# High and low value parts side by side in one attention matmul, added by VectorE

## The chip, the cores and the metric

The kernel runs on one core of a Trainium2 chip. The metric is device time of one launch in microseconds (us). TensorE (PE in the profile), VectorE (DVE), ScalarE (ACT), GpSimd (POOL) and SyncE (SP, here only a queue of transfers) each run their own instruction list and meet at semaphores.

## The reference

One decoder layer over 1024 rows of width 1024, in float32: attention, then an MLP, then a gated embedding. Only the attention is touched:

```python
q, k, v = split(rmsnorm(x, g) @ wqkv)          # 16 query heads, 4 key/value heads, head width 64
q, k = rmsnorm(q, gq), rmsnorm(k, gk)
# blocks of 128 rows; block n sees the keys of blocks n-1 and n, window 128
probs = exp(scores - m) / (sum + exp(sink - m))
o = einsum('bnkgqs,bnskd->bnqkgd', probs, vb)  # the step that the change rewrites
mix = o.reshape(b, s, H * HD) @ wo
```

The output has to agree with a float32 computation, so every operand of a matmul is split into a high part (rounded to the engine's fp32r type) and a low part (the rest), and a product is three matmuls: high x high, high x low, low x high.

## The kernel before

The attention is worked off in 8 blocks n of 128 rows. Each has four steps j, one for each key/value head with its four query heads; (n, j) is one step. The whole program is written by hand: each engine has its own list, a semaphore stands between any two that hand something on, and blocks 1 to 5 are a loop in every list. Blocks 0, 6 and 7 are written out.

What TensorE does in step j of block n: `scores` of (n, j); a piece of the projections of block n+1 (`project`, L1919: "q0" and "q8" are the two halves of the queries, "k" is keys and values); `weigh_values` (L1990, the product of probabilities and values) two steps behind, so of (n, j-2); and `turn_probs` (L1969, transposes) of (n, j-1). In step 3 it starts `project("q8")` of the next block, which waits until VectorE has scaled the keys (L1326), since "k" and "q8" share a PSUM bank. That start is called the **gate** below, since it comes once in a block.

VectorE in a step: `add_bias` (L1374, L1387, L1392: masks and biases the scores and takes their maximum), the step's share of the norms (L1308 sums of squares, L1321 and L1326 scaling) and of the low parts (L1301, L1344, L1335), `scale_probs` (L1404), and then `pT_lo_part` (L1410, low part of the turned probabilities of the step before). In step 0 `v_diff` (L1354) follows, in step 1 `v_lo_part` (L1360 and L1363, the low parts of the block's values and of their difference to the block before).

ScalarE: `exps` (L938, waits for the maxima), squares (L891), high parts (L928 queries, L920 keys, L947 probabilities), and `attention_out` (L955), which copies the finished 128x256 product of (n, j-2) out of its PSUM bank just ahead of `pT_hi_part` (L947).

GpSimd: the inverse square roots (L691, L693), the mask on the turned probabilities (`mask_probs`, L760 for the high part, L763 for the low), and `dv_hi_part` (L737), the high part of the difference of values. In its list `dv_hi_part` stands behind `head_norm("q0")` of the next block. VectorE's L1363 waits for it.

The values lie in `vz` as [slot, part, head, 64] with zeros between the heads, so that 128 columns from it hold one head's 64 values and 64 zeros, on either side. Twelve matmuls of 256 columns make one product: two slots (this block's values and the difference), three passes, and two placements. The upper 64 partitions of the bank take two of the four query heads and the lower 64 the other two. The bank `pv_bank` is used by all steps in turn, so the product of the next step waits for `attended`, which the copy signals.

Of the kernel before, what the change touches and what calls it, by code (L numbers as in the profile page):

```python
# [30 lines left out]
P = 128  # L31
# [30 lines left out]
def trunk_layer(nc, x, p, mix_g, mlp_g, ple_g, wqkv, gq, gk, sinks, wo, w1, w2, w_proj, w_gate, out):  # L62
# [31 lines left out]
    with ExitStack() as ctx:  # L94
# [55 lines left out]
        vz = sb("vz", [P, 2, 2, (2 * KV + 1) * HD], F32R, in_a)  # L150
# [168 lines left out]
        half_ready = sem("half_ready")  # L319
# [14 lines left out]
        gain_zero = sem("gain_zero")  # L334
# [33 lines left out]
        pv_done = sem("pv_done")  # L368
        attended = sem("attended")
# [293 lines left out]
        def _(pool):  # L663
            pool.memset(gain[:, 0:2 * P], 0.0).then_inc(gain_zero, 1)
            pool.memset(half[:], -0.5).then_inc(half_ready, 1)
# [4 lines left out]
            pool.wait_ge(half_ready, 1)  # L670
# [24 lines left out]
            pool.memset(vz[:].bitcast(F32), 0.0).then_inc(zeros_ready, 1)  # L695
# [49 lines left out]
            def dv_hi_part(b):  # L745
# [4 lines left out]
                copy(vz[:, 0, HI, HD:(2 * KV + 1) * HD].rearrange("p (v a d) -> p v a d", v=KV, a=2)[:, :, 0, :],  # L750
# [23 lines left out]
            def body(n, last=False):  # L774
# [61 lines left out]
        def _(act):  # L836
# [65 lines left out]
            def values(slot, s):  # L902
                return vz[:, slot, s, HD:(2 * KV + 1) * HD].rearrange("p (v a d) -> p v a d", v=KV, a=2)[:, :, 0, :]

            def v_hi_part(b):
                act.wait_ge(v_staged, b + 1)
                if isinstance(b, int) and b == 0:
                    act.wait_ge(zeros_ready, 2)

                wait(act, pv_done, 4 * b)  # L910
                nc.scalar.activation(values(1, HI), vnext[:].rearrange("p (v d) -> p v d", v=KV),
                                     ACT.Copy).then_inc(v_hi, 1)
# [36 lines left out]
            def attention_out(n, j):  # L949
# [91 lines left out]
            act.wait_ge(gain_zero, 1)  # L1041
# [5 lines left out]
            act.wait_ge(half_ready, 1)  # L1047
# [236 lines left out]
        def _(dve):  # L1284
# [63 lines left out]

            def v_diff(b):
                dve.wait_ge(v_staged, b + 1)  # L1350
                if isinstance(b, int) and b == 0:
                    dve.wait_ge(zeros_ready, 3)
# [3 lines left out]
            def v_lo_part(b):  # L1356
                def values(slot, s):
                    return vz[:, slot, s, HD:(2 * KV + 1) * HD].rearrange("p (v a d) -> p v a d", v=KV, a=2)[:, :, 0, :]
# [949 lines left out]
```

## Time and profile before

| | us |
|---|---|
| median of three runs | 1116.42 |
| lowest and highest | 1115.62, 1116.71 |
| the profiled execution | 1118.16 |
| its span in the trace | 1116.4 |
| attention, start to the gate of block 7 | 246.3 |
| one block of the loop, gate to gate | 31.4 |

The profiled execution took 1.8 us more than its span, and 1.7 us more than the median. A difference worked out in the trace is taken over to the median as it is. Times below are us from the start of the span. A row of a timeline or of the chain is: start, length, engine, line, operation, output<-input and shape, how many; in brackets how long the engine stood idle before and who ended that.

### The profile page before, as it was taken

The numbers are of one execution on the slowest core, as the hardware profiler recorded it, in microseconds if no ns is written. First come the engines' busy times: TensorE is split into PE (matmuls) and PEld (weight loads), VectorE is DVE, ScalarE is ACT, GpSimd is POOL, SyncE is SP. The second block draws the span as 40 slices with busy tenths as digits, with TensorE's granted clock in tenths as the row PEclk, the third lists the DMA queues.
The fourth block names the chain that finished last, engine by engine and source line by source line (L and its number), as shares of the span: only waits on it lengthen the run. The fifth ranks groups of instructions, "written<-read, shape, count | busy, mean of one in ns | idle before, by whom it ended". The sixth has DMA issues, their size and how long they took to land.

```text
span 1116.4 us, 14894 instructions
## 1 busy us (share of the span) xinstructions
PE 1089.0 (98%) x5272; PEld 913.1 (82%) x5272; DVE 735.2 (66%) x1130; ACT 428.2 (38%) x776; POOL 148.9 (13%) x272
## 2 busy tenths in 40 slices
PE   7899999998999999999999999999999999999998
PEld 5788888887888888888888888888888888888886
DVE  6677776777544499876677667498777863664311
ACT  7456555565423233313322343453333331243100
POOL 6543444443100000000000000000000000010000
PEclk9999999998999999999999999999999999999999
DMA  7000000121152407343353244998888872111210
GB/s 264 20 20 19 19 1 19 38 111 79 38 170 80 147 1 256 139 171 132 119 201 139 88 188 164 396 411 297 293 287 294 282 250 76 38 38 57 88 45 38
DMA packets 61361, 153.88 MB, mean 138 GB/s; under 512 B 4720, under 2 KB 5752, under 8 KB 61304
## 3 DMA queue, kind: packets, MB, share of 16 engines
q1 hardware_dynamic: 61280, 153.12, 38.4%
q8 instruction: 35, 0.57, 0.2%
q14 instruction: 22, 0.18, 0.1%
q10 hardware_dynamic: 24, 0.01, 0.0%
HBM read 119.03 MB, written 34.08 MB: 137 GB/s over the span
## 4 chain that ended last, share of the span: by engine, by line
PE 81%; DVE 8%; issue 4%; ACT 3%; POOL 2%; ACTq 0%; DVEq 0%; POOLq 0%
PE pair L2204 24%; PE pair L2184 21%; PE pair L2056 8%; PE pair L2247 8%; PE pair L1919 6%; PE pair L2224 4%; PE pair L2142 3%; PE pair L1990 2%; PE pair L2260 2%; ACT probs L938 2%; PE pair L2112 1%; PE pair L1958 1%; DVE probs L1387 1%; ACT kn L891 1%; POOL k_rstd L693 1%
## 5 line engine op out<-in xcount | busy, mean ns | idle before, releaser
L2204 PE MATMUL pair<-uT 128*128 128x512 f32 x1176 | 266.7, 389 | 0.0
L2204 PEld LDWEIGHTS pair<-uT 128*128 128x128 f32 x1176 | 220.7, 188 | 45.8
L1919 PE MATMUL pair<-WA,xT 128*128 128x512 f32 x384 | 97.4, 403 | 11.8 <-DVE kn L1326 7.8
L1193 ACT ACTIVATE uT<-wo_raw 128x1024 fp32r<-128x1024 f32 x63 | 64.3, 1055 | 105.7 <-PE pair L2204 92.7
L1735 DVE TENSOR_TENSOR uT<-wo_raw,uT 128x1024 fp32r<-128x1024 f32 x63 | 75.0, 1222 | 39.3 <-ACT uT L1193 39.2
L675 POOL TENSOR_SCALAR row_var<-row_ssq 128x1 f32<-128x1 f32 x16 | 3.1, 193 | 700.3 <-ACT hn L1092 700.3
L1919 PEld LDWEIGHTS pair<-WA,xT 128*128 128x128 f32 x384 | 70.7, 191 | 29.3 <-issue 13.2
L2056 PE MATMUL pair<-WA,oT 128*128 128x512 f32 x384 | 91.8, 397 | 2.6 <-DVE WA L1491 2.1
L2056 PEld LDWEIGHTS pair<-WA,oT 128*128 128x128 f32 x384 | 72.2, 191 | 17.8 <-issue 3.1
L2184 PE MATMUL pair<-WA,WB 128*128 128x512 f32 x336 | 78.2, 389 | 0.4 <-ACT xr L1168 0.4
L2184 PEld LDWEIGHTS pair<-WA,WB 128*128 128x128 f32 x336 | 63.0, 188 | 13.8 <-DVE WB L1669 0.8
L938 ACT ACTIVATE probs<-probs,nmax 128x129 f32<-128x129 f32 x128 | 50.0, 393 | 59.8 <-DVE nmax L1392 59.6
L2184 PE MATMUL pair<-uT,WB 128*128 128x512 f32 x240 | 56.1, 389 | 0.0
L1990 PE MATMUL pair<-pT,vz 128*128 128x256 f32 x384 | 53.3, 289 | 0.5 <-DVE pT L1410 0.5
L2184 PEld LDWEIGHTS pair<-uT,WB 128*128 128x128 f32 x240 | 45.0, 188 | 9.6 <-issue 0.2
L1990 PEld LDWEIGHTS pair<-pT,vz 128*128 128x128 f32 x384 | 50.4, 194 | 2.2 <-DVE pT L1410 0.7
L1867 DVE TENSOR_TENSOR act_buf<-pair,act_buf 128x512 f32<-128x512 f32 x16 | 11.0, 690 | 55.3 <-PE pair L2260 55.3
L1919 PE MATMUL pair<-WB,xT 128*128 128x512 f32 x192 | 45.3, 391 | 2.1 <-DVE WB L1292 2.1
L1826 DVE TENSOR_TENSOR RES<-RES,pair 128x512 f32<-128x512 f32 x48 | 30.8, 682 | 22.2 <-PE pair L2204 22.2
L2224 PE MATMUL pair<-WA 128*128 128x512 f32 x192 | 45.4, 393 | 0.0
L2247 PE MATMUL pair<-WB,uT 128*128 128x512 f32 x192 | 45.2, 391 | 0.0
L2247 PE MATMUL pair<-WA,uT 128*128 128x512 f32 x192 | 44.8, 389 | 0.0
(203 smaller groups left out, 1877.9 us busy)
## 6 DMA issues: line engine op xcount, KB each, us to landing
wo_raw<-in_m_w SPq DMA_DIRECT2D x53, 512.0 KB, 6.5
wo_raw<-hid_kept SPq DMA_DIRECT2D x36, 512.0 KB, 4.7
hid_kept<-RES SPq DMA_DIRECT2D x28, 512.0 KB, 2.6
emb<-in_m_w SPq DMA_DIRECT2D x20, 512.0 KB, 6.2
RES<-in_m_w SPq DMA_DIRECT2D x8, 1024.0 KB, 6.8
uT_f<-in_m_w SPq DMA_DIRECT2D x6, 1024.0 KB, 6.7
act_buf<-hid_kept SPq DMA_DIRECT2D x11, 512.0 KB, 4.9
hn<-in_m_w SPq DMA_DIRECT2D x11, 512.0 KB, 5.9
```

The costliest lines, as they stand in the source:

```text
L938: ex = nc.scalar.activation(row, row, ACT.Exp, bias=nmax[:, i, r:r + 1], accum_out=denom[:, i, r:r + 1])
L1193: nc.scalar.activation(operand(t, which, HI), unit(t, which), ACT.Copy).then_inc(op_hi, 1)
L1735: nc.vector.tensor_tensor(operand(t, which, LO), unit(t, which), operand(t, which, HI).bitcast(F32), ALU.subtract).then_inc(op_ready, 1)
L1826: nc.vector.tensor_tensor(RES[:, b, cols], RES[:, b, cols], bank[:], op).then_inc(posted, 1)
L1919: mm = nc.tensor.matmul(proj_bank[X][:], xT[:, s, kt, :], w[:, m, kt, at:at + BANK], start=(kt == 0 and i == 0), stop=(kt == KT - 1 and i ...
L1990: mm = nc.tensor.matmul(pv_bank[:, 0:2 * P], vz[:, kt, s, at:at + 2 * HD], pT[:, m, kt, odd * 2 * P:(odd + 1) * 2 * P], start=(done == 0), ...
L2056: mm = nc.tensor.matmul(out_bank(b, odd, c)[:], oT[:, hf, s, k % 4 * P:(k % 4 + 1) * P], wo_s[:, m, k, c * BANK:(c + 1) * BANK], start=(k ...
L2142: mm = nc.tensor.matmul(ps[i % 4][:], w1_s[:, s, kt, m * P:(m + 1) * P], uT[:, r, kt, th * BANK:(th + 1) * BANK], start=(kt == 0 and q == ...
L2184: mm = nc.tensor.matmul(chain[:, m, :], a_slot[q % 4][:, s, k, m * P:(m + 1) * P], right(i)(r)[:, k, :], start=(opens and k == 0 and n == ...
L2204: mm = nc.tensor.matmul(ps[4 * (j % 2) + m][:], operand(t, 0, s)[:, k, m * P:(m + 1) * P], operand(t, 1, r)[:, k, :], start=(g == 0 and k ...
L2224: mm = nc.tensor.matmul(ps[4 + a % 4][:], hid[:, s, k, b * P:(b + 1) * P], w2_s[:, r, k, c * BANK:(c + 1) * BANK], start=(k == 0 and q == ...
L2247: mm = nc.tensor.matmul(ps[4 + s % 2][:], uT[:, u, kt, b * P:(b + 1) * P], w[:, m, kt, :], start=(kt == 0 and q == 0), stop=(kt == KT - 1 ...
```

## The change

- `vz` becomes [slot, head, part, 64]: a head's high and low values stand side by side, and the zeros are gone (with GpSimd's clearing of `vz`). Filler keeps the other tiles where they were.
- `weigh_values` issues four matmuls of 512 columns: slot x {high, low part of the probabilities}. The upper 64 partitions of the bank then hold the product with the high values, the lower 64 that with the low values, for all four query heads. The product low x low, which was left out, is in it.
- ScalarE copies the upper half out in two instructions of 64x256: the second writes to the lower 64 partitions of RES. VectorE's new `add_lows` adds the lower half of the bank to it, also in two instructions of 64x256. It stands behind `pT_lo_part` in each step, and signals `attended`.
- In GpSimd's `body`, `dv_hi_part` moves ahead of `head_norm("q0")`. Block 0 keeps its order.
- Two semaphores of the start become one.

```diff
-                copy(vz[:, 0, HI, HD:(2 * KV + 1) * HD].rearrange(...)[:, :, 0, :],
+                copy(vz[:, 0, :, HI, :],
                      vprev[:].rearrange("p (v d) -> p v d", v=KV)).then_inc(dv_moved, 1)
...
                 place_sinks(n, 2)
+                dv_hi_part(n)
                 if not last:
                     head_norm("q0", n + 1)
-                dv_hi_part(n)
...
-                nc.scalar.activation(dst, pv_bank[:, 0:2 * P], ACT.Copy).then_inc(attended, 1)
+                nc.scalar.activation(dst[0:HD, :], pv_bank[0:HD, 0:2 * P], ACT.Copy)
+                nc.scalar.activation(dst[HD:P, :], pv_bank[0:HD, 2 * P:4 * P], ACT.Copy).then_inc(pv_copied, 1)
...
+            def add_lows(n, j):
+                dve.wait_ge(pv_copied, 4 * n + (j + 1))
+                dst = RES[:].rearrange("p b n -> p (b n)")[:, bass.ds(n * D + j * 2 * P, 2 * P)]
+                nc.vector.tensor_tensor(dst[0:HD, :], pv_bank[HD:P, 0:2 * P], dst[0:HD, :], ALU.add)
+                nc.vector.tensor_tensor(dst[HD:P, :], pv_bank[HD:P, 2 * P:4 * P], dst[HD:P, :],
+                                        ALU.add).then_inc(attended, 1)
...
                     if not (first and j < 1):
                         pT_lo_part(t - 1, (j - 1) % 2)
+                    if not (first and j < 2):
+                        add_lows(*before(n, j, 2))
...
-                    for s, m in PASSES:
-                        for odd in range(2):
-                            at = 2 * HD * j + (0 if odd else HD)
-                            mm = nc.tensor.matmul(pv_bank[:, 0:2 * P], vz[:, kt, s, at:at + 2 * HD],
-                                                  pT[:, m, kt, odd * 2 * P:(odd + 1) * 2 * P],
-                                                  start=(done == 0), stop=(done == 11))
-                            done += 1
+                    for m in (HI, LO):
+                        mm = nc.tensor.matmul(pv_bank[:], vz[:, kt, j, :, :].rearrange("p s d -> p (s d)"),
+                                              pT[:, m, kt, :], start=(done == 0), stop=(done == 3))
+                        done += 1
```

On VectorE, step 1 of the loop, before: the scaled probabilities, the low part of the turned ones, and the two low parts of the values.

```order
L1404 TENSOR_TENSOR probs<-probs,rden 128x4x128
L1410 TENSOR_TENSOR pT<-pair,pT 128x512
L1360 TENSOR_TENSOR vz<-vnext,vz 128x4x64
L1363 TENSOR_TENSOR vz<-vprev,vz 128x4x64
L431 ISA
L1374 COPY_PREDICATED pair<-current,pair 128x2x128
```

The same place after the change:

```order
L1410 TENSOR_TENSOR probs<-probs,rden 128x4x128
L1416 TENSOR_TENSOR pT<-pair,pT 128x512
L1348 REGISTER_ALU
L1350 ISA
L1350 TENSOR_TENSOR RES<-pair,RES 64x256
L1351 ISA
L1351 TENSOR_TENSOR RES<-pair,RES 64x256
L1366 TENSOR_TENSOR vz<-vnext,vz 128x4x64
L1369 TENSOR_TENSOR vz<-vprev,vz 128x4x64
L432 ISA
L1380 COPY_PREDICATED pair<-current,pair 128x2x128
```

Two additions stand between the low part of the probabilities and what followed it; steps 0, 2 and 3 have them at the same place.

On GpSimd, in the middle of the loop, before (vz<-vprev is `dv_hi_part`):

```order
L771 TENSOR_SCALAR probs<-sink 128x4
L691 TENSOR_SCALAR q_var<-q_ssq,row_eps 128x8
L693 TENSOR_TENSOR q_rstd<-q_var,half 128x8
L737 TENSOR_SCALAR vz<-vprev 128x4x64
L760 AFFINE_SELECT pT<-pT 128x512
```

And after:

```order
L771 TENSOR_SCALAR probs<-sink 128x4
L737 TENSOR_SCALAR vz<-vprev 128x4x64
L692 TENSOR_SCALAR q_var<-q_ssq,row_eps 128x8
L694 TENSOR_TENSOR q_rstd<-q_var,half 128x8
L760 AFFINE_SELECT pT<-pT 128x512
```

The copy now comes ahead of the norm of the queries instead of behind it.

## Rows read from the trace of the kernel before

**Rows 1.** The page, part 1: busy time of TensorE over the span.
```profile
PE 1089.0 (98%) x5272; PEld 913.1 (82%) x5272; DVE 735.2 (66%) x1130; ACT 428.2 (38%) x776; POOL 148.9 (13%) x272
```

**Rows 2.** Busy time, blocks 1 and 3, gate to gate: stretch, length, engines' busy, PEclk, DMA.
```profile
56.28:89.36 33.08, 31.93 (x189) 28.08 (x189) 22.77 (x73) 17.56 (x55) 15.15 (x28) 0.95 0.05 17
120.80:152.25 31.45, 30.30 (x188) 26.94 (x189) 22.87 (x73) 17.46 (x55) 14.04 (x24) 1.00 0.05 17
```

**Rows 3.** The chain, gate of block 3 to the next: start, length, what.
```profile
130.66 1.44 PE pair L1990 x12
...
133.48 3.43 PE pair L1919 x15
...
142.52 0.70 DVE pT L1410
...
145.54 0.48 DVE pair L1374 x2
```

**Rows 4.** Timeline around the values' low parts and xT, block 3.
```profile
131.84 1.29 DVE L1301 TENSOR_TENSOR xT<-pair,xT 128x512 fp32r<-128x512 f32 x2
...
133.32 3.59 PE L1919 MATMUL pair<-WA,xT 128*128 128x512 f32 x15
...
143.13 0.41 DVE L1360 TENSOR_TENSOR vz<-vnext,vz 128x256 fp32r<-128x256 f32 x1
...
144.78 0.83 DVE L1363 TENSOR_TENSOR vz<-vprev,vz 128x256 fp32r<-128x256 f32 x1 [1.24 <-POOL vz L737]
```

**Rows 5.** Timeline of VectorE and ScalarE after the gate at 152.25.
```profile
152.83 0.68 DVE L1410 TENSOR_TENSOR pT<-pair,pT 128x512 fp32r<-128x512 f32 x1
153.44 0.75 DVE L1374 COPY_PREDICATED pair<-current,pair 128x256 f32<-128x256 uint32 x2
...
157.07 0.69 ACT L920 ACTIVATE kT<-pair,columns 128x512 fp32r<-128x512 f32 x1
...
158.62 0.39 ACT L955 ACTIVATE RES<-pair 128x256 f32 x1 [0.87 <-PE pair L1990]
...
158.92 0.60 ACT L947 ACTIVATE pT<-pair 128x512 fp32r<-128x512 f32 x1
159.55 0.69 DVE L1410 TENSOR_TENSOR pT<-pair,pT 128x512 fp32r<-128x512 f32 x1 [0.78 <-ACT pT L947]
...
160.94 0.69 DVE L1308 TENSOR_REDUCE q_ssq<-kn 128x8 f32<-128x512 f32 x1 [0.70 <-ACT kn L891]
```

**Rows 6.** Timelines: runs on the same partitions, runs that change them; maxima of step 1.
```profile
13.85 2.81 DVE L1292 SCALAR_TENSOR_TENSOR WA<-RES,columns,WA 128x512 fp32r<-128x512 f32 x4 [0.26 <-ACT WA L846]
...
16.11 2.55 ACT L846 ACTIVATE WA<-RES,columns 128x512 fp32r<-128x512 f32 x4
...
137.07 0.16 DVE L1392 SCALAR_TENSOR_TENSOR nmax<-rmax,nsink 128x4 f32<-128x4 f32 x1
...
137.47 1.39 ACT L928 ACTIVATE qT<-pair,gq_s 64x512 fp32r<-64x512 f32 x2 [2.10 <-PE pair L1943]
...
155.39 1.53 DVE L1344 SCALAR_TENSOR_TENSOR qT<-pair,gq_s,qT 64x512 fp32r<-64x512 f32 x2
```

**Rows 7.** Timeline of TensorE in block 7: a wait, and what follows.
```profile
269.42 2.90 PE L2056 MATMUL pair<-WA,oT 128*128 128x512 f32 x6 [2.06 <-DVE WA L1491]
...
272.12 2.76 PE L1990 MATMUL pair<-pT,vz 128*128 128x256 f32 x12
...
274.68 1.74 PE L2056 MATMUL pair<-WA,oT 128*128 128x512 f32 x6
```

**Rows 8.** Busy time in stretches ahead of a gate: PE busy second, PEclk third from the end.
```profile
53.20:56.28 3.08, 0.72 (x5) 0.45 (x5) 1.82 (x5) 2.37 (x7) 1.90 (x3) 1.00 0.00 0
...
150.40:152.25 1.85, 0.70 (x6) 0.45 (x5) 0.80 (x3) 1.05 (x3) 1.59 (x2) 1.00 0.00 0
```

**Rows 9.** Timeline of GpSimd at the start.
```profile
1.77 2.02 POOL L695 MEMSET vz<- 128x2304 f32 x1
...
12.77 0.21 POOL L682 TENSOR_SCALAR row_var<-row_ssq 128x1 f32<-128x1 f32 x1 [3.95 <-ACT xn L867]
```

More of the change, by code:

```diff
@@ L149, in trunk_layer @@
         vnext = sb("vnext", [P, KV * HD], F32, in_a)
-        vz = sb("vz", [P, 2, 2, (2 * KV + 1) * HD], F32R, in_a)
+        vz = sb("vz", [P, 2, KV, 2, HD], F32R, in_a)
+        sb("after_vz", [P, 1280], F32, in_a)
         pT = sb("pT", [P, 2, 2, BANK], F32R, in_a)
@@ L318, in trunk_layer @@
         ident_ready = sem("ident_ready")
-        half_ready = sem("half_ready")
         zeros_ready = sem("zeros_ready")
@@ L333, in trunk_layer @@
         x_eps = sem("x_eps")
-        gain_zero = sem("gain_zero")
+        small_filled = sem("small_filled")
         heads_in = sem("heads_in")
@@ L368, in trunk_layer @@
         pv_done = sem("pv_done")
+        pv_copied = sem("pv_copied")
         attended = sem("attended")
@@ L663, in _ @@
         def _(pool):
-            pool.memset(gain[:, 0:2 * P], 0.0).then_inc(gain_zero, 1)
-            pool.memset(half[:], -0.5).then_inc(half_ready, 1)
+            pool.memset(gain[:, 0:2 * P], 0.0).then_inc(small_filled, 1)
+            pool.memset(half[:], -0.5).then_inc(small_filled, 1)
             pool.memset(ident[:], 0.0).then_inc(ident_ready, 1)
@@ L669, in _ @@
                                base=0, pattern=[[-1, P]], channel_multiplier=1).then_inc(ident_ready, 1)
-            pool.wait_ge(half_ready, 1)
+            pool.wait_ge(small_filled, 2)
             def row_norm(squares, var_sem, rstd_sem, b):
@@ L749, in dv_hi_part @@
                     stand(pool, pv_done, 4 * b)
-                copy(vz[:, 0, HI, HD:(2 * KV + 1) * HD].rearrange("p (v a d) -> p v a d", v=KV, a=2)[:, :, 0, :],
+                copy(vz[:, 0, :, HI, :],
                      vprev[:].rearrange("p (v d) -> p v d", v=KV)).then_inc(dv_moved, 1)
@@ L900, in stage_v @@
                                      scale=row_rstd[:]).then_inc(v_staged, 1)
-            def values(slot, s):
-                return vz[:, slot, s, HD:(2 * KV + 1) * HD].rearrange("p (v a d) -> p v a d", v=KV, a=2)[:, :, 0, :]
             def v_hi_part(b):
                 act.wait_ge(v_staged, b + 1)
-                if isinstance(b, int) and b == 0:
-                    act.wait_ge(zeros_ready, 2)
                 wait(act, pv_done, 4 * b)
-                nc.scalar.activation(values(1, HI), vnext[:].rearrange("p (v d) -> p v d", v=KV),
+                nc.scalar.activation(vz[:, 1, :, HI, :], vnext[:].rearrange("p (v d) -> p v d", v=KV),
                                      ACT.Copy).then_inc(v_hi, 1)
@@ L1039, in oT_hi_half @@
                 nc.scalar.activation(oT[:, hf, HI, :], src, ACT.Copy).then_inc(oT_hi, 1)
-            act.wait_ge(gain_zero, 1)
+            act.wait_ge(small_filled, 1)
             act.dma_start(gain[0:KT, 0:P], mix_g.rearrange("(k p) -> k p", p=P)).then_inc(gain_in, 16)
@@ L1045, in _ @@
                               g.partition_broadcast(2).unsqueeze(0)).then_inc(heads_in, 16)
-            act.wait_ge(half_ready, 1)
+            act.wait_ge(small_filled, 2)
             nc.scalar.activation(warm[:], half[:, 0:1], ACT.Exp)
@@ L1347, in q_lo_part, with before @@
                     op1=ALU.subtract).then_inc(T_ready[X], 1)
+            def add_lows(n, j):
[4 more added lines that the diff above has]
+                                        ALU.add).then_inc(attended, 1)
+            def before(n, j, lag):
+                return (n, j - lag) if j >= lag else (n - 1, j - lag + GROUPS)
             def v_diff(b):
@@ L1351, in v_diff @@
                 if isinstance(b, int) and b == 0:
-                    dve.wait_ge(zeros_ready, 3)
+                    dve.wait_ge(zeros_ready, 2)
                 wait(dve, dv_moved, 2 * b)
@@ L1422, in last_part @@
                     v_diff(n)
+                    add_lows(n - 1, 2)
                 if j == 1:
@@ L1428, in last_part @@
                     v_lo_part(n)
+                    add_lows(n - 1, 3)
                     wo_lo_unit(2)
@@ L1434, in last_part @@
                     pT_lo_part(t - 1, (j - 1) % 2)
+                    add_lows(n, 0)
                     wo_lo_unit(4)
@@ L1438, in last_part @@
                     pT_lo_part(t - 1, (j - 1) % 2)
+                    add_lows(n, 1)
                     wo_lo_unit(5)
@@ L1533, in _ @@
             pT_lo_part(NB * GROUPS - 1, 1)
+            add_lows(NB - 1, 2)
             oT_lo_half(1, 1)
@@ L1570, in _ @@
             add_attention(0, False)
+            add_lows(NB - 1, 3)
             oT_lo_half(2, 0)
```

11 lines of the change are left out of this document (4 added, 7 removed).

## The prediction

> **What bounds the kernel now.** I read the page first. TensorE is busy 98% of the span [rows 1], so the 12 matmuls that become 4 look like a plain gain. The second view, busy time by block, says how much of that holds in the attention: a block takes 31.45 us and TensorE is busy in 30.30 of them [rows 2]. The rest is one wait at the gate. The third view, the chain of waits, says what sets the gate [rows 3]. A block has two stages. In the first, from the gate at 120.80 [rows 2] to the turn of the queries "q8", the chain lies on TensorE. In the second it leaves TensorE: ScalarE takes the turned queries, then come exponentials, squares, VectorE (L1410 at 142.52), GpSimd's copy, VectorE again (`add_bias` at 145.54) [rows 3], exponentials and key norm, up to the gate at 152.25. A matmul saved in the second stage buys nothing, while each VectorE instruction between 142.52 and 145.54 costs its full length. The reader is also to see that the first stage is TensorE's by a hair only: the low parts of xT end at 131.84 + 1.29 = 133.13, and the projection that needs them starts at 133.32 [rows 4]. So VectorE is at the edge in both stages, and it is VectorE that gets the new work.
>
> **Removed: eight of twelve matmuls.** Twelve took 1.44 us in the chain [rows 3], 0.12 each. A matmul of 512 columns took 3.43 / 15 = 0.229 [rows 3], so four take 0.92 and each product gets 0.52 shorter: 32 products, 16.6 us of TensorE's time. Two of the four in a block lie in the first stage, at most 1.04 there, and the other two lie beside the second.
>
> **Added: the pair of additions.** No row shows a 64x256 addition. Its own length is taken from L1360, 128x256, 0.41 [rows 4]; lines of this kernel take time by columns, not by partitions. What matters is how close it can follow its neighbour. From below: L1360's class starts the next one 0.34 later (my estimate, from L1410 to L1374, which start 0.61 apart at a length of 0.68 [rows 5], so 0.07 overlap), and a pair costs 0.68. From above: L1344, two instructions that swap the halves of the partitions, took 1.53 for two of 0.75 [rows 6], so the second starts 0.78 after the first and there is no overlap but a gap of 0.03; L1292 has the same operation and columns, stays on all partitions, and took 2.81 for four, 0.69 apart. `add_lows` swaps halves at each of its steps: its first reads the lower half of PSUM behind a full-height L1410, its second reads and writes the lower half of RES, and what follows is back at the top. So I take the upper value: L1410 costs 0.72 and not 0.61, each addition 0.45, together **1.01 a pair**. ScalarE shows the same: L928 with swapped halves 1.39 for two, 0.70 apart, L846 on all partitions 2.55 for four, 0.62 apart [rows 6]. So its two copies cost 0.39 each where one cost 158.92 - 158.62 = 0.30 [rows 5], 0.48 more.
>
> The Trainium skill has a rule that speaks against the change here: in "VectorE: DVE Perf Modes", section "Two Vector instructions with no wait between them", an instruction whose input or output starts in another group of 32 partitions than the one before is held until everything before it has finished. The trace agrees (0.78 against 0.69 apart). By the rule the sum is the one I make; without it, it is the first rival's.
>
> **First stage, with the additions.** From the gate at 152.25 [rows 5]: the pair of (n, 0) comes behind L1410 at 152.83, so L1374 goes from 153.44 to 154.45, and the exponentials and the keys' high part on ScalarE from 157.07 to 158.08. ScalarE is free 0.62 later, at 158.70. The product was ready 0.52 earlier, at 158.10, which is no longer what is late. Two copies, 0.78: L947 starts at 159.48, not 158.92. L1410 starts at 160.11, not 159.55, and with 0.61 + 1.01 behind it L1308 starts at 161.73, not 160.94. VectorE's idle 0.78 and 0.70 are used up and **0.79** is left over. It reaches TensorE through xT, since there was no slack (133.13 to 133.32). The third pair of the stage, in step 0, has cover: the maxima for step 1 are there at 137.07, and ScalarE is busy with the queries until 137.47 + 1.39 = 138.86 [rows 6], 1.8 later; the pair and the longer copies use 1.0 + 0.5 of it.
>
> **Second stage.** GpSimd's copy now needs only the product of (n-1, 3) and `v_diff`, both long done, so the wait of 1.24 ahead of L1363 goes [rows 4]. What is late next is VectorE itself: L1360 starts 1.01 later, at 144.14, L1363 at 144.47 and, still beside GpSimd's mask, takes 0.76 to the next: `add_bias` starts at 145.23, not 145.54, **-0.31**. ScalarE's longer copies cost nothing here: VectorE runs through from the squares' sums to L1410 at 142.52 [rows 3], and does not stand waiting for it.
>
> The length of L1363 has two bounds: 0.83 as now, or 0.41 like its twin L1360 [rows 4]. The Trainium skill, "GPSIMD Engine Reference", section "1. Specifications", says that GpSimd shares its SBUF interfaces with VectorE instructions that have two SBUF inputs, which is L1363's case; the trace agrees in that only the one of the two that starts with GpSimd's mask takes 0.83. GpSimd's mask moves to the same moment as before, so I take 0.83.
>
> **The sum.** A block: +0.79 - 0.31 = +0.48. Six periods lie between the gate at 56.28 and block 7's at 246.3. The first ran partly at half clock (33.08 us, clock 0.95 [rows 2]), TensorE is the later one in its first stage, and I take +0.1 - 0.31 = -0.2. Five others: +2.4. Block 7: three pairs, 3.0, stand on VectorE before the third low part of WO (L1491), which TensorE waits 2.06 for [rows 7]. Behind that TensorE is the bound, at half clock first: the product took 274.68 - 272.12 = 2.56, and four matmuls at the (272.12 - 269.42) / 6 = 0.45 of the six before it take 1.80 [rows 7], -0.76; two more save 0.52 each, so 3.0 - 1.8 = +1.2. The last product lies beside the turn of oT on ScalarE and VectorE, no gain; the last additions lie beside the output projection. The clearing of `vz`, 2.02, had 3.95 of idle time behind it [rows 9]: nothing. Block 0 has its first additions behind the key norm, nothing before its gate. Together -0.2 + 2.4 + 1.2 = **+3.4**. The profiled execution would be 1118.16 + 3.4 = 1121.6; the median is 1116.42 + 3.4 = **1119.8**. Nothing after the attention changes: TensorE's list is the same there.
>
> **Rivals.**
> 1. *The additions and copies overlap like full-height neighbours* (faster). A pair is 0.68, the copies 0.27 each. First stage: ScalarE is ready for L947 at 158.91, L1410 starts at 159.54 and L1308 at 160.83, -0.11. Second: -1.24 + 0.68 = -0.56. Five blocks of -0.67, block 1 -1.0 (half of TensorE's saving arrives there), block 7 3 x 0.68 - 1.8 = +0.2: -4.1, **1112.3**. For it: no row has this very form. Against it: [rows 6]. Chance 0.22.
> 2. *The copy's move also frees L1363 from the mask* (about no change). It takes 0.41: another -0.41 in six blocks, -2.5, **1117.3**. For it: GpSimd's list is shorter ahead of it. Against: the norm of the queries still ends where it did, and the mask follows at once. Chance 0.18.
> 3. *TensorE's clock falls in each block* (slower). Work pauses longer ahead of the gate. In block 0 a stretch of 3.08 us with 0.72 busy, four transposes, was followed by a fall to half clock; 1.85 us with 0.70 busy was not [rows 8]. With the products shorter that stretch becomes some 2.4 us, between the two. A fall cost 33.08 - 31.45 = 1.63 [rows 2], of which some 0.67 is covered where VectorE is late anyway: 0.96 in five blocks, +4.8, **1124.6**. It decides from the point where the pause of 2.4 counts as the 3.08 did. Chance 0.12.
> 4. *The moved copy does not help* (slower): it stands in GpSimd's list waiting for the product of (n-1, 3), and the norm of the queries queues behind it. Then 1.24 comes back in six blocks, +7.4, **1127.2**. The product stands on TensorE ahead of all that L1410 at 142.52 [rows 3] waits for, so I give it 0.03.
>
> **How the numbers follow.** My forecast has 0.45. It is uncertain by about 0.3 a block, 1118 to 1122. 0.2%, 2.2 us, is about what a measurement of this kernel can tell from no change, so "same" is 1114.2 to 1118.6. Faster: rival 1, and little else, 0.24. Same: rival 2 and the low end of my forecast, 0.26. Slower: the rest of it, rivals 3 and 4, 0.50. The range has to hold rival 1 and one or two falls of the clock: 1110.5 to 1125.0, which leaves out the upper half of rival 3, rival 4 and a larger gain. Were the additions as long as L1344's 0.78, the upper end of any row, the time would pass 1128; were they hidden altogether, both stages would give all they have, 1.04 + 1.24 a block, and it would be near 1102.
>
> **What would show it.** Four matmuls of L1990's successor 0.23 apart. Additions that start 0.42 or more apart (0.34: rival 1). No idle time on VectorE before L1308 of "q8", and TensorE waiting for xT or for `add_bias` in steps 0 and 1. The wait of 1.24 gone. Blocks of 31.9 us (30.8: rival 1; 31.5: rival 2), and no clock below 1.00 between 100 and 240. I am wrong if the additions fall into idle time of VectorE that I take to be used up.

## The result, and the profile after

The changed kernel takes 1128.5 us (median of five runs, 1126.22 to 1128.8), beside 1116.42 before: ratio 1.0106, 95% interval 1.0092 to 1.012. It is 12 us slower. The forecast was 1119.8 with a range to 1125.0, so the sign was right and the time was outside the range.

The profiled execution was the fastest of the five, 1126.22, with a mean granted clock of 0.992; three of the others had 0.989. Its span is 1124.5, so 8.1 us longer than that of before. First the page: the busy times, and the clock in 40 slices (the last row, in tenths of full speed).

```profile
PE 1081.3 (96%) x5016; PEld 891.5 (79%) x5016; DVE 766.6 (68%) x1194; ACT 441.8 (39%) x808; POOL 145.0 (13%) x271
...
PEclk9999999998999999999999999999999999999999
```

TensorE has 256 matmuls less and is busy only 7.7 us less than in [rows 1]. By line, the products are 17.0 us shorter (53.3 to 36.3), as forecast, but the same 384 matmuls of the projections take 101.2 instead of 97.4: most of that is paid at half clock. The rest of the difference was not followed up. VectorE has 64 instructions more. The next view is the timeline of TensorE, cut to the gates of blocks 1 to 4 and 7: start, length, line, and in brackets the wait ahead and who ended it.

```profile
56.27 5.96 PE L1933 MATMUL pair<-WA,xT 128*128 128x512 f32 x18 [1.04 <-DVE kn L1323]
...
89.44 4.37 PE L1933 MATMUL pair<-WA,xT 128*128 128x512 f32 x18 [1.15 <-DVE kn L1323]
...
121.57 5.95 PE L1933 MATMUL pair<-WA,xT 128*128 128x512 f32 x18 [1.15 <-DVE kn L1323]
...
154.81 4.33 PE L1933 MATMUL pair<-WA,xT 128*128 128x512 f32 x18 [1.15 <-DVE kn L1323]
...
251.05 7.31 PE L1933 MATMUL pair<-WA,xT 128*128 128x512 f32 x24 [1.04 <-DVE kn L1323]
```

Read the differences of the starts. 121.57 - 89.44 = 32.13, against 31.45 before [rows 2]: a block of the loop is 0.68 us longer, not 0.48. 154.81 - 121.57 = 33.24: in this block the same 18 matmuls took 5.95 instead of 4.33. The view of busy time by stretch says why (stretch, length, busy time of PE, PEld, DVE, ACT, POOL with counts, PEclk, DMA share, GB/s):

```profile
89.44:121.57 32.13, 29.18 (x157) 24.06 (x157) 26.84 (x81) 19.14 (x59) 14.20 (x24) 1.00 0.05 16
121.57:154.81 33.24, 30.52 (x156) 25.27 (x157) 26.84 (x81) 19.37 (x59) 14.19 (x24) 0.95 0.04 16
...
184.37:186.95 2.58, 0.66 (x4) 0.45 (x5) 1.52 (x5) 2.27 (x6) 1.90 (x3) 1.00 0.00 0
119.00:121.57 2.57, 0.66 (x6) 0.45 (x5) 1.51 (x5) 2.26 (x6) 1.90 (x3) 1.00 0.00 0
```

The clock is 0.95 over that block: it fell to half, 1.2 GHz, at its gate. Ahead of the gate TensorE had been busy 0.66 us in 2.57; before the change it was 0.70 in 1.85 [rows 8]. The same stretch ahead of the gate at 186.95 was not followed by a fall, so the fall is not certain each time. It came at 121.57 (1.1 us) and at 251.05 (24 matmuls in 7.31 instead of 5.72, 1.6 us). The fall at block 1's gate, 56.27, is no news: the kernel before has it too [rows 2].

The waits of TensorE between 60 and 260 (engine, line, who ended them, sum, times, longest):

```profile
PE pair L1933 <- DVE kn L1323: 6.8, 6, 1.2
PE pair L1957 <- DVE qn L1318: 4.6, 6, 0.8
```

The first is the wait at the gate, as before. The second, ahead of the turn of the queries "q0", is new: 0.8 in each of six blocks. Last, VectorE and GpSimd where the forecast had its terms, after the gate at 186.95 and around the values' low parts:

```profile
187.53 0.68 DVE L1416 TENSOR_TENSOR pT<-pair,pT 128x512 fp32r<-128x512 f32 x1
188.25 0.43 DVE L1350 TENSOR_TENSOR RES<-pair,RES 64x256 f32 x1
188.69 0.43 DVE L1351 TENSOR_TENSOR RES<-pair,RES 64x256 f32 x1
189.15 0.76 DVE L1380 COPY_PREDICATED pair<-current,pair 128x256 f32<-128x256 uint32 x2
...
196.41 0.69 DVE L1305 TENSOR_REDUCE q_ssq<-kn 128x8 f32<-128x512 f32 x1
197.13 0.76 DVE L1380 COPY_PREDICATED pair<-current,pair 128x256 f32<-128x256 uint32 x2
...
211.49 0.85 DVE L1369 TENSOR_TENSOR vz<-vprev,vz 128x256 fp32r<-128x256 f32 x1
212.37 0.76 DVE L1380 COPY_PREDICATED pair<-current,pair 128x256 f32<-128x256 uint32 x2
...
211.32 0.74 POOL L760 TENSOR_SCALAR_AFFINE_SELECT pT<-pT 128x512 fp32r<-128x512 f32 x1
```

The additions start 0.72 behind L1416 and 0.44 apart, and the next starts 0.46 later: 1.62 from L1416 to L1380, against 0.61 before [rows 5], so a pair costs 1.01. L1369 has no wait any more [rows 4], and takes 0.85 beside GpSimd's mask, which started 0.17 before it.

| part of the profiled execution | forecast | measured | of it half clock |
|---|---|---|---|
| block 1 (56.27 to 89.44) | -0.2 | +0.1 | 0 |
| five blocks | +2.4 | +4.6 | 1.1 |
| block 7, gate to the last part of the output projection | +1.2 | +3.4 | 1.6 |
| the rest | 0 | 0.0 | |
| sum | +3.4 | +8.1 | 2.7 |

Block 7 is 302.80 - 251.05 = 51.75 against 294.71 - 246.33 = 48.38.

### The profile page after: what moved, and what is told of

The parts are those of the page before. It is cut to its first block, busy times and chain, and to the rows that moved or that the text cites. A ratio compares the mean times of both kernels' runs of the same rounds, so it can differ in the third digit from the quotient of the medians.

```text
span 1124.5 us, 14546 instructions
## 1 busy us (share of the span) xinstructions
PE 1081.3 (96%) x5016; PEld 891.5 (79%) x5016; DVE 766.6 (68%) x1194; ACT 441.8 (39%) x808; POOL 145.0 (13%) x271
## 4 chain that ended last, share of the span: by engine, by line
PE 71%; DVE 7%; ACT 2%; issue 2%; POOL 0%; DVEq 0%; ACTq 0%; POOLq 0%
PE pair L2216 24%; PE pair L2196 21%; PE pair L2259 8%; PE pair L2068 7%; PE pair L2236 4%; PE pair L2154 3%; PE pair L2272 2%; PE pair L2124 1%; ACT probs L933 1%; DVE probs L1393 1%; PE pair L1933 1%; DVE pair L1380 0%; DVE RES L1736 0%; DVE RES L1351 0%; PE pair L2003 0%
## 5 line engine op out<-in xcount | busy, mean ns | idle before, releaser
L1933 PE MATMUL pair<-WA,xT 128*128 128x512 f32 x384 | 101.2, 414 | 13.1 <-DVE kn L1323 7.8
L1972 PE MATMUL pair<-kT,qT 128*128 128x256 f32 x256 | 38.4, 292 | 9.0 <-DVE rmax L1393 7.9
L1261 ACT ACTIVATE act_buf<-pair 128x512 f32<-128x512 f32 x16 | 9.6, 598 | 89.7 <-PE pair L2259 84.0
L2196 PE MATMUL pair<-WA,slot_ring 128*128 128x512 f32 x192 | 44.8, 389 | 0.0
```

Of the source, the lines that this page charges most:

```text
L1933: mm = nc.tensor.matmul(proj_bank[X][:], xT[:, s, kt, :], w[:, m, kt, at:at + BANK], start=(kt == 0 and i == 0), stop=(kt == KT - 1 and i ...
L1972: mm = nc.tensor.matmul(dst, qT[:, G * j + r, :], kT[:, m, j, :, :].rearrange("p a n -> p (a n)"), start=(m == HI), stop=(m == LO))
L2196: mm = nc.tensor.matmul(chain[:, m, :], a_slot[q % 4][:, s, k, m * P:(m + 1) * P], right(i)(r)[:, k, :], start=(opens and k == 0 and n == ...
```

## The experiments

Two theories were to be told apart. **Theory H**: VectorE is held where the additions change the half of the partitions; that holds up both stages. **Theory C**: the loss is TensorE's clock, which falls behind the longer pause. Their rivals were the length of the additions as such, ScalarE's copies, and the product's form. All times are medians; the ratio to the kernel before, measured on the same chip, has its interval beside it.

### One part alone: the move of GpSimd's copy

```diff
                 place_sinks(n, 2)
+                dv_hi_part(n)
                 if not last:
                     head_norm("q0", n + 1)
-                dv_hi_part(n)
```

> The kernel before with one edit: GpSimd's dv_hi_part stands ahead of head_norm("q0") in the body. Theory A (the gain of the change is this move, and the additions ate it): the wait of 1.24 us ahead of L1363 goes, nothing else becomes late, L1374 starts some 0.9 to 1.2 earlier in step 1 of each block, a block takes 30.3 to 30.5 us instead of 31.45, and the time is 1110 to 1112. Theory B (TensorE, busy 30.30 of 31.45 in a block, or ScalarE takes the place of the wait): at most 0.5 a block, 1113.5 or more. In the changed kernel the second stage became shorter by only 0.16 where the move should give 1.24 and two additions take 1.0; under A this run shows 0.9 to 1.2 for the move alone.

Measured: **1110.05**, ratio 0.9947 (0.9929 to 0.9964), faster than before. VectorE in step 1:

```profile
200.27 0.41 DVE L1360 TENSOR_TENSOR vz<-vnext,vz 128x256 fp32r<-128x256 f32 x1
200.61 0.42 DVE L1363 TENSOR_TENSOR vz<-vprev,vz 128x256 fp32r<-128x256 f32 x1
200.94 0.75 DVE L1374 COPY_PREDICATED pair<-current,pair 128x256 f32<-128x256 uint32 x2
```

The wait of 1.24 is gone, and L1363 takes 0.42 and no longer 0.83, because it now lies ahead of the mask (which starts at 201.47). A block is (238.36 - 56.89) / 6 = 30.2 us, no gate behind that of block 1 waits for VectorE, and TensorE is the bound:

```profile
149.00:179.00 30.00, 29.94 (x189) 26.70 (x188) 22.09 (x72) 17.45 (x55) 13.88 (x24) 1.00 0.06 17
```

The opposite run, the change without its move:

```diff
-                dv_hi_part(n)
                 if not last:
                     head_norm("q0", n + 1)
+                dv_hi_part(n)
```

> The changed kernel without the move of GpSimd's copy: dv_hi_part stands behind head_norm("q0") again. Theory A (VectorE reaches L1369 of the changed kernel so late, behind its two additions, that the copy is almost there anyway): L1369 waits 0.2 to 0.4 in a block, the time is 1129 to 1131. Theory B (the move is worth the 1.24 us that VectorE waited before): 6 x 1.24 more, 1135 to 1136.

Measured: **1130.4**, ratio 1.0123 (1.0106 to 1.0141).

```profile
214.94 0.83 DVE L1369 TENSOR_TENSOR vz<-vprev,vz 128x256 fp32r<-128x256 f32 x1 [0.30 <-POOL vz L737]
```

Theory A of that run holds: behind two additions the copy is late by only 0.30, and a block without a fall is 189.05 - 156.57 = 32.48, 0.35 longer. So the one edit is worth 6 us alone and 2 us beside the additions: they stand just where the wait was.

### The additions taken away

```diff
             def add_lows(n, j):
-                dve.wait_ge(pv_copied, 4 * n + (j + 1))
...
+                return
...
-                nc.scalar.activation(dst[HD:P, :], pv_bank[0:HD, 2 * P:4 * P], ACT.Copy).then_inc(pv_copied, 1)
+                nc.scalar.activation(dst[HD:P, :], pv_bank[0:HD, 2 * P:4 * P], ACT.Copy).then_inc(attended, 1)
```

> The changed kernel without VectorE's additions: ScalarE's second copy signals that the bank is free. The product with the low parts of the values is left out. Theory A (the additions are the cost, by the time they hold VectorE): each block gets back 2 x 0.8 to 1.0 on its chain, until TensorE itself bounds it; a block takes about 29.6 us, and the time is 1108 to 1113, without half clock ahead of block 7 but for block 1's. Theory B (ScalarE's longer copies or the product in a whole bank are the cost): a block stays above 31 us and the time above 1120.

Measured: **1102.67**, ratio 0.9877 (0.9859 to 0.9895), and 29.2 us a block, below the range that I had given. The forecast had said "near 1102" for additions that are hidden altogether. So the product's new form and ScalarE's longer copies are not the loss. The additions cost 26 us. The 64 of them are busy for 27, but not all of the 26 is their own time on the path. Without them the subtraction L1369 starts 0.86 ahead of the mask and takes 0.42, so 2.6 us (0.43 in each of six blocks) go to the mask beside which they push it, and the clock takes a part too. The next runs take these apart.

### The change of half

Three runs keep two additions of 64x256 in each step and change only where they read and write; `spare` is the filler tile behind `vz`. All three leave out the low parts' sum in RES. First, all in the upper half:

```diff
-                nc.vector.tensor_tensor(dst[0:HD, :], pv_bank[HD:P, 0:2 * P], dst[0:HD, :], ALU.add)
-                nc.vector.tensor_tensor(dst[HD:P, :], pv_bank[HD:P, 2 * P:4 * P], dst[HD:P, :],
+                nc.vector.tensor_tensor(spare[0:HD, 0:2 * P], pv_bank[0:HD, 0:2 * P], dst[0:HD, :], ALU.add)
+                nc.vector.tensor_tensor(spare[0:HD, 2 * P:4 * P], pv_bank[0:HD, 2 * P:4 * P], dst[0:HD, :],
```

> The changed kernel with both additions on the upper 64 partitions alone: they read the upper half of the bank and of RES and write to the filler tile, each 64x256 as before, so VectorE does the same number of instructions of the same size, but none changes partitions. The sum with the low parts of the values is left out. Theory A (an instruction that changes the half of the partitions can't overlap the one before it): the additions start 0.34 apart and not 0.44, a pair takes 0.68 to 0.75 of VectorE and not 1.03, a block 31.5 to 31.7 us, and the time is 1123 to 1126. Theory B (64x256 additions take 0.44 wherever they stand, because they read PSUM): no difference, 1127.5 to 1129.5.

Measured: **1111.43**, ratio 0.9961 (0.9947 to 0.9975), far below both expectations.

```profile
179.17 0.68 DVE L1416 TENSOR_TENSOR pT<-pair,pT 128x512 fp32r<-128x512 f32 x1
179.77 0.40 DVE L1350 TENSOR_TENSOR after_vz<-pair,RES 64x256 f32<-64x256 f32 x1
180.10 0.40 DVE L1351 TENSOR_TENSOR after_vz<-pair,RES 64x256 f32<-64x256 f32 x1
180.43 0.74 DVE L1380 COPY_PREDICATED pair<-current,pair 128x256 f32<-128x256 uint32 x2
...
187.25 0.67 DVE L1305 TENSOR_REDUCE q_ssq<-kn 128x8 f32<-128x512 f32 x1
187.85 0.74 DVE L1380 COPY_PREDICATED pair<-current,pair 128x256 f32<-128x256 uint32 x2
...
201.82 0.41 DVE L1369 TENSOR_TENSOR vz<-vprev,vz 128x256 fp32r<-128x256 f32 x1
...
202.03 0.70 POOL L760 TENSOR_SCALAR_AFFINE_SELECT pT<-pT 128x512 fp32r<-128x512 f32 x1
```

The distances are 0.60, 0.33 and 0.33, the pair costs 0.66, as the first rival had it. But the block is 30.27 us, 1.86 shorter than the change's. Three pairs lie on the chain, two in the first stage and one in the second, and explain 3 x 0.35. Most of the rest stands in the same rows. VectorE reaches L1369 0.21 ahead of the mask instead of 0.17 behind it, and it takes 0.41: 0.44 saved. And L1380 comes 0.60 behind L1305, where the change has 0.72; behind L1369 the change loses 0.12 in the same way (0.88, where it was 0.76 [rows 4]). Some 0.1 us is left over. Outside of this block there is another gain: the pauses are shorter, and the gates have no falls after the first.

This run differed from the change in two things, the half and the tile written. The next keeps the halves of the change and writes to the filler tile:

```diff
+                nc.vector.tensor_tensor(spare[0:HD, 0:2 * P], pv_bank[HD:P, 0:2 * P], dst[0:HD, :], ALU.add)
+                nc.vector.tensor_tensor(spare[HD:P, 2 * P:4 * P], pv_bank[HD:P, 2 * P:4 * P], dst[HD:P, :],
```

> The changed kernel with the additions' result written to the filler tile instead of RES, the halves as in the change: the first reads the lower half of the bank and the upper of RES and writes the upper half, the second reads the lower half of both and writes the lower. The low parts of the values are left out of RES. It stands between the change and the run with both additions on the upper half, which differed from the change in two things, the half and the tile written. Theory A (the change of half is the price): as the change, additions 0.44 apart, 0.72 behind L1416, a block of 32.1 us, 1126 to 1129. Theory B (writing RES in place is the price): as the run on the upper half, 0.33 apart, 30.3 us, 1111.

Measured: **1126.47**, ratio 1.0088 (1.0069 to 1.0106); 120.59 - 88.47 = 32.12 us a block, additions 0.44 apart, half clock at 152.71, 218.06 and 251.07. Writing RES in place is not the price; what is left is the half on which the additions read and write. The third run crosses from the lower to the upper half in both additions alike:

```diff
+                nc.vector.tensor_tensor(spare[0:HD, 0:2 * P], pv_bank[HD:P, 0:2 * P], dst[0:HD, :], ALU.add)
+                nc.vector.tensor_tensor(spare[0:HD, 2 * P:4 * P], pv_bank[HD:P, 2 * P:4 * P], dst[0:HD, :],
```

> The same, but both additions read the lower half of the bank and the upper half of RES and write the upper half of the filler tile: each crosses from one half to the other, but the two are alike. The low parts of the values are left out. Theory A (an instruction is held by what differs from its neighbour): the first starts 0.72 behind L1416 and the next instruction 0.44 behind the second, but the second 0.33 behind the first, a pair of 0.92 instead of 1.03, a block 31.6 to 31.9 us, 1124 to 1127. Theory B (each instruction whose inputs lie in different halves is held, whatever stands ahead of it): all three distances as in the change, 32.1 us a block, 1126 to 1129. Theory C (only the output's half counts, which never changes here): 0.33 throughout and 30.3 us a block, 1111.

Measured: **1117.41**, ratio 1.0003 (0.9993 to 1.0013), 31.11 us a block.

```profile
191.52 0.69 DVE L1416 TENSOR_TENSOR pT<-pair,pT 128x512 fp32r<-128x512 f32 x1 [0.30 <-ACT pT L942]
192.25 0.43 DVE L1350 TENSOR_TENSOR after_vz<-pair,RES 64x256 f32<-64x256 f32 x1
192.59 0.42 DVE L1351 TENSOR_TENSOR after_vz<-pair,RES 64x256 f32<-64x256 f32 x1
192.93 0.68 DVE L1305 TENSOR_REDUCE q_ssq<-kn 128x8 f32<-128x512 f32 x1
193.64 0.76 DVE L1380 COPY_PREDICATED pair<-current,pair 128x256 f32<-128x256 uint32 x2
```

The first addition is held (0.73), the second is not (0.34): an instruction is held by what differs from an earlier one, not by crossing halves itself, so Theory B of this run falls. So does Theory C: the output's half never changes here, and the first is held. The time came out below Theory A's 1124 to 1127, since L1369 got ahead of the mask here too (0.06 before it, rows in the last section).

### The clock

Extra matmuls that nobody reads, put into TensorE's two waits:

```diff
+            def filler(n, count):
+                pe.wait_ge(T_ready["q8"], 2 * n + 2)
+                for i in range(count):
+                    nc.tensor.matmul(ps[6][:], xT[:, HI, i, :], wq_q[:, HI, i, 0:BANK], start=True, stop=True)
...
                     if j == 3 and not last:
+                        filler(n, 3)
                         turn_q("q0", n + 1)
+                        filler(n, 4)
```

> The changed kernel with extra matmuls of 128x512 that nobody reads, in step 3 of blocks 0 to 6: three ahead of the turn of the queries "q0", four ahead of the gate. They lie in TensorE's two waits of the changed kernel (0.8 and 1.15 us), so that it works on through them: 49 matmuls, 11 us more work for TensorE. Theory A (part of the loss is TensorE's clock, which falls behind a longer pause): no half clock at the gates but perhaps the first, the granted clock of the runs is 0.995 or more where the changed kernel has 0.989 to 0.992, and the time is 1121 to 1124.5, faster with more work. Theory B (the falls are there in any case, or cost nothing where VectorE is late): the same 1127 to 1129.5 or more.

Measured: **1122.24**, ratio 1.0051 (1.0036 to 1.0065), with a clock of 0.996 or 0.997 in all runs. TensorE has 49 matmuls more, and the kernel is 6.3 us faster than the change (6.1 by the two ratios, since the two were measured on different chips).

```profile
56.08 4.09 PE L1933 MATMUL pair<-WA,xT 128*128 128x512 f32 x17
...
88.24 4.37 PE L1933 MATMUL pair<-WA,xT 128*128 128x512 f32 x18 [0.22 <-DVE kn L1323]
...
181.91 0.86 PE L1980 MATMUL pair<-WA,xT 128*128 128x512 f32 x3
182.85 0.65 PE L1957 MATMUL pair<-ident,qn 128*128 128x128 f32 x4
183.26 1.17 PE L1980 MATMUL pair<-WA,xT 128*128 128x512 f32 x4
184.65 4.34 PE L1933 MATMUL pair<-WA,xT 128*128 128x512 f32 x18 [0.22 <-DVE kn L1323]
...
56.00:250.00 194.00, 186.11 (x984) 151.83 (x985) 163.45 (x485) 116.43 (x351) 86.31 (x148) 1.00 0.07 25
```

The clock is 1.00 from 56 to 250, and a block is 32.13 us, as the change's undisturbed ones. So this run is the change with its falls up to block 7's gate taken out, and the 6.3 between it and the change are the clock's. It is still 5.7 us over the kernel before (by the ratio). Those 5.7 are not all that VectorE costs, since this run has also lost the fall in block 1, which the kernel before keeps: block 1 takes 88.24 - 56.08 = 32.16 here, 33.17 in the change and 33.08 before. Of the 12 us that the change is slower, then, some 6.3 - 1.0 = 5.3 are falls that it added, and some 6.7 are VectorE's. Then each piece alone, the three ahead of the turn and the four ahead of the gate.

```diff
                         filler(n, 3)
                         turn_q("q0", n + 1)
-                        filler(n, 4)
```

> The changed kernel with the three extra matmuls ahead of the turn of the queries alone; the gate keeps its wait of 1.15 us. With all seven the time was 1122.24, and without 1128.5. Theory A (what the clock answers to is the whole thin stretch ahead of the gate: 2.6 us with 0.66 busy in the changed kernel, 1.85 with 0.70 in the kernel before, 2.1 with 0.66 in the run with the values' low parts first, which had no fall there): either filling alone makes it thick enough, no half clock at the gates 2 to 7, 1121.5 to 1124. Theory B (the longest single pause decides, the one at the gate): no help, 1126.5 to 1129.

```diff
-                        filler(n, 3)
                         turn_q("q0", n + 1)
                         filler(n, 4)
```

> The changed kernel with the four extra matmuls ahead of the gate alone; the turn of the queries keeps its wait of 0.8 us. Theory A (the whole thin stretch counts) and B (the longest pause, at the gate) both expect no half clock at the gates 2 to 7 and 1121.5 to 1124. Theory C (the pause ahead of the turn, which the kernel before did not have, decides by itself): no help, 1126.5 to 1129, and the run with three alone is the one at 1122.

Measured: **1123.61**, ratio 1.0064 (1.005 to 1.0078), and **1123.05**, ratio 1.0059 (1.0045 to 1.0072). In neither profile was there half clock at the gates 2 to 7. The first still has the pause of 1.15 at the gate, the second the pause of 0.8 ahead of the turn. So in these runs neither pause does it by itself; the falls came where both stood, with only 0.66 of work between them.

### Other places for the additions

The values' low parts ahead of the additions in step 1:

```diff
+                    if j == 1:
+                        v_lo_part(n)
                     if not (first and j < 2):
                         add_lows(*before(n, j, 2))
                     if j == 0:
                         v_diff(n)
-                    if j == 1:
-                        v_lo_part(n)
```

> The changed kernel with one exchange in VectorE's step 1: the values' low parts (L1366, L1369) ahead of the two additions instead of behind them. In the changed kernel L1369 started at 211.49, 0.17 after GpSimd's mask (211.32), and took 0.85; with the additions on the same half it started 0.21 ahead of the mask and took 0.41. Theory A (it is slow only beside the mask): it starts 0.9 earlier, takes 0.42, the additions come beside the mask with their one input from PSUM and keep 0.43, a block takes 31.7 us, and the time is 2.5 us less, 1125 to 1126.5. Theory B (the long time is that of a form with two inputs behind the additions, or moves to the additions): a block stays at 32.1 and the time at 1127.5 to 1129.5.

Measured: **1121.14**, ratio 1.0036 (1.0022 to 1.005). That is 7.4 us less than the change, by the exchange of two neighbours in a list, and 4 us below what Theory A gave.

```profile
207.15 0.42 DVE L1366 TENSOR_TENSOR vz<-vnext,vz 128x256 fp32r<-128x256 f32 x1
207.48 0.42 DVE L1369 TENSOR_TENSOR vz<-vprev,vz 128x256 fp32r<-128x256 f32 x1
207.93 0.43 DVE L1350 TENSOR_TENSOR RES<-pair,RES 64x256 f32 x1
...
181.90:183.99 2.09, 0.66 (x5) 0.45 (x5) 1.04 (x4) 1.79 (x4) 1.74 (x3) 1.00 0.00 0
```

L1369 takes 0.42, and the additions keep 0.43, the second of them beside the mask (which starts at 208.34). A block is 31.63, 0.50 less, some 3 us in six. The other 4 us are put down to the clock, as what is left over: the stretch ahead of a gate is 2.09 us and no longer 2.58, and none of the gates 2 to 7 is at half clock in the profile. I had left that out of the expectation.

Then all pairs moved away from L1416, but for the one that the product of step 0 needs:

```diff
                     add_bias(n, j, first)
+                    if not (first and j < 3) and j > 0:
+                        add_lows(*before(n, j, 3))
...
                         pT_lo_part(t - 1, (j - 1) % 2)
-                    if not (first and j < 2):
-                        add_lows(*before(n, j, 2))
+                    if j == 3:
+                        add_lows(n, 1)
```

> The changed kernel with the same additions in other places of VectorE's list: the pair of (n, j-3) right behind add_bias in steps 1 to 3, and that of (n, 1) at the end of step 3. None stands any more between the low part of the probabilities and what waits behind it in steps 0 to 2; the same in block 7. Theory A (the additions cost by the place, where VectorE is on the chain): a block is 30.2 to 31.0 us and the time 1108 to 1116. Theory B (a pair takes 1.0 us of VectorE's time and pushes the chain wherever it is): a block stays at 32.1 and the time within 2 us of 1128.5. Theory C (the product then waits for its bank): TensorE shows a new wait ahead of the product, and the time is above 1128.

Measured: **1114.86**, ratio 0.9983 (0.9972 to 0.9995). A block is 30.07, 2.06 less than the change's and 1.38 less than before: the place decides. L1369 takes 0.42 there, ahead of the mask. In block 7, where `last_part` was changed in the same way, a longer wait of the product for its bank took part of it back, Theory C's in that block alone (the change waits 1.38 for it there, at 262.97):

```profile
260.26 2.04 PE L2005 MATMUL pair<-pT,vz 128*128 128x512 f32 x4 [4.32 <-DVE RES L1351]
```

The last run keeps the moved pairs in blocks 0 to 6, and in block 7 moves only the pair of (6, 3):

```diff
                     v_lo_part(n)
-                    add_lows(n - 1, 3)
                     wo_lo_unit(2)
+                    add_lows(n - 1, 3)
                     wo_lo_unit(3)
```

> The whole computation. Blocks 0 to 6 as in the run with late additions, where a block took 30.07 us. Block 7 as in the change, but with the pair of (6, 3) behind the third low part of WO instead of ahead of it. Theory (block 7 lost 2.9 us for three pairs ahead of that low part, and the late additions lost more there, because the product waited 4.3 us for its bank): the gate of block 7 at 238.0, from there to the last product's output projection 49 us instead of 54 with late additions, and 1109 to 1111.5, about the time of the kernel before with GpSimd's copy moved (1110.05). The rival (the additions are needed before the third low part, the product waits): as the late additions, 1113 to 1115.

Measured: **1110.64**, ratio 0.9944 (0.9928 to 0.996). It is the whole computation and faster than the kernel before, and level with the move alone (1110.05, ratio 0.9947). Block 7 took 289.76 - 239.48 = 50.3 us in its profile, which had half clock there at 249.83. So the product's new form, in the places that I found for its additions, brings nothing that these runs can tell over the old form with the move.

## Why the prediction was wrong

**Right: the bound, the pair and the first stage.** VectorE at the edge was the right place to look. The pair costs 1.01 as forecast; ScalarE's copies take 0.77 together, forecast 0.78. L1305 of "q8" starts 9.46 behind its gate (196.41 - 186.95); the working had 161.73 - 152.25 = 9.48. The wait of 1.24 went, and L1369 stayed beside the mask, so rival 2 did not come, nor rival 1. Both are real mechanisms, though: with the halves alike they appear together, and the time is 1111.43. The rule from the Trainium skill on which the upper value rested ("VectorE: DVE Perf Modes", section "Two Vector instructions with no wait between them") held, with 0.44 against 0.33 apart. But the prediction told it too narrowly, as a comparison with the one before. The Trainium skill keeps SBUF and PSUM apart there: it compares where an input starts with the last instruction that read the same memory, and where the output starts with the last that wrote it, however many stand between.

**Too small: the two stages, by 0.2 a block.** "-0.31" of the second stage was -0.16, and +0.79 of the first was +0.85 at the exponentials. The rows show where: L1305 to L1380 is 0.72, where it is 0.60 with the additions in the upper half (187.25 to 187.85 in that run); L1369 to L1380 is 0.88, where I took the 0.76 of [rows 4]. In both, L1380 stands one or two instructions behind the additions, and still comes 0.11 to 0.12 late. I had counted the hold at the additions and at their direct neighbour. By the rule as the Trainium skill has it, L1380 is held too, since it is the first behind the additions that reads PSUM, and it starts in the upper half. The trace agrees: two such holds make 0.23 a block, about the missing 0.2, and 1.1 in five.

**Too small: block 7, by 0.6 without its fall.** "3.0" for three pairs was right (278.62 - 251.05 - 1.59 = 25.98 against 23.09 before, +2.9). The gain behind them was 1.1 and not 1.8. TensorE waits 0.83 for the maxima at 290.98, a wait that before does not have, and 0.83 instead of 0.30 for the low part of oT at 302.80: "TensorE is the bound" from there on no longer held once the pairs of steps 2 and 3 stood on VectorE. TensorE's timeline of the changed kernel:

```profile
278.62 2.90 PE L2068 MATMUL pair<-WA,oT 128*128 128x512 f32 x6 [2.75 <-DVE WA L1503]
...
290.98 3.02 PE L2068 MATMUL pair<-WA,oT 128*128 128x512 f32 x12 [0.83 <-DVE rmax L1393]
...
302.80 2.55 PE L2068 MATMUL pair<-WA,oT 128*128 128x512 f32 x10 [0.83 <-DVE oT L1508]
```

Block 1's -0.2 was +0.1, mostly for the first reason.

**The step that failed: the sum has no term for falls of the clock.** They took 2.7 us of the profiled execution, and some 5.3 over the runs (filled pauses, less block 1's). Without them the profiled execution would be 5.4 longer than before and not 8.1, and the time inside the range, as it is with the pauses filled (1122.24). Rival 3 had the mechanism, and its price of 0.96 a fall was near the measured 1.1: "That stretch becomes some 2.4 us, between the two." It became 2.58, since VectorE was later than worked out and since a pause of 0.8 opened ahead of the turn, which the working of the gate did not have: I shortened TensorE's work and moved VectorE's back, and never set the two against each other at the turn of "q0". I gave the rival 0.12, as a fall in each block. The falls come in some blocks, at 1.1 us in the loop and 1.6 at block 7. The range made room for one or two, but above a forecast whose VectorE part was itself too small: 3.4, where the profile has 5.4 and the medians some 6.7. The prediction's own sign, no clock below 1.00 between 100 and 240, failed at 121.57.

What stays open: when one of two equal stretches is followed by half clock. The stretches ahead of 121.57 and 186.95 differ by 0.01 us, and only the first was. In the change without its move the pauses are longer, and the gates at 89.38, 122.98, 189.05 and 222.52 are at half clock, while that at 156.57 is not.

## What to carry to other kernels

Where two engines share the bound, a saving on the one and a load on the other open a pause between them, and on TensorE the pause has a second price, since its clock may halve behind it. Look for the thin stretches ahead of each wait and see whether the edit makes them longer.

An edit that bundles a gain with a loss hides both. Here the move of one small copy was worth 6 us by itself, and two neighbours exchanged in the list of the changed kernel 7; neither could be seen in the sum.

Where a hold depends on the partitions that were used last, price the instructions further down the list too, up to the next one that uses the same memory.

## What the hardware showed that was not expected

- **A hold reaches past the neighbour.** Where both additions read the lower half of PSUM and write the upper half of SBUF, the instructions behind them that work in SBUF alone start on time (L1305, 0.34 behind), and the next one that works on PSUM, L1380, starts 0.71 behind L1305 instead of 0.60. That is the comparison by memory told of above: the start in PSUM against that of the last instruction that used PSUM, and that in SBUF apart from it. In the same run L1380 starts 0.44 behind L1369, which is itself not held, instead of 0.34. No run was made for this alone.
- **A mask on GpSimd doubles a subtraction on VectorE, by who starts first.** L1369 took 0.85 where it started 0.17 behind the mask, and 0.41 where it started 0.21 ahead, although half of it was beside the mask. That is the same in the loop's blocks of each run: 0.83 to 0.86 where it starts 0.07 to 0.17 behind the mask, 0.41 or 0.42 where it starts ahead. With both additions crossing alike it started 0.06 ahead, and it was the mask that took longer (0.86, where 0.64 is its usual time):

```profile
207.78 0.42 DVE L1369 TENSOR_TENSOR vz<-vprev,vz 128x256 fp32r<-128x256 f32 x1
...
207.84 0.86 POOL L760 TENSOR_SCALAR_AFFINE_SELECT pT<-pT 128x512 fp32r<-128x512 f32 x1
```

The second addition, which has one input in PSUM, took 0.43 beside the mask in the run with the low parts first.
- **More work made the kernel faster**: with 49 matmuls that nobody reads, 1122.24 where the change took 1128.5.
